# Second layer's gates activated in three sets (three, two and three) in place of four pairs

## The reference

```python
def odd_layer(x, norm_g, w_in, w_out, qn, kn, lq1, lk1, lq2, lk2, subln_g, cos, sin, lambda_init):
    h = rms_norm(x, norm_g)
    proj = h @ w_in
    q, k, v, gate = jnp.split(proj, [C_QK, 2 * C_QK, 2 * C_QK + C_W], axis=-1)   # 8 heads
    ...                                   # q and k: normalised, halves rotated; two scores a head
    o = differential_attention(q1, q2, k1, k2, v, lam)
    o = rms_norm(o, subln_g) * (1.0 - lambda_init)
    y = (o.reshape(b, s, C_W) * jax.nn.silu(gate)) @ w_out
    return x + y
```

## Time and profile before

| | |
|---|---|
| median of 3 runs | 1946.0 us (1945.42 to 1946.75) |
| the profiled execution's own time | 1947.44 us |
| its span in the trace | 1945.5 us |
| TensorE matmuls busy | 1916.6 us, 99% |
| VectorE busy | 1039.5 us, 53% |
| ScalarE busy | 999.3 us, 51% |
| GpSimd busy | 953.6 us, 49% |
| table loads on ScalarE | 37, of 1.283 us each |

### The profile page before, as it was taken

How to read it: one execution, slowest core, us unless ns; L and a number is a source line. 1 busy time by engine, 2 the same in 40 slices (tenths; PEclk the granted TensorE clock), 3 DMA queues, 4 the chain that set the end, 5 groups by cost and what they waited for, 6 DMA issues and landing times.

```text
span 1945.5 us, 27030 instructions
## 1 busy us (share of the span) xinstructions
PE 1916.6 (99%) x10082; PEld 1600.7 (82%) x10082; DVE 1039.5 (53%) x1882; ACT 999.3 (51%) x1767; POOL 953.6 (49%) x1238
## 2 busy tenths in 40 slices
PE   9999999999999999999999999999999999999998
PEld 7888787788788888888888888888878888888887
DVE  4376545756636766776565644312556574444214
ACT  5477546676725556665345444422656364444323
POOL 5642167555444444444555555555534355555553
PEclk9999999999999999999999999999999999999999
DMA  5321123322222222222222322333222122223332
GB/s 202 102 73 52 41 87 109 87 82 81 76 87 86 77 77 76 68 77 74 92 93 87 103 98 98 92 97 96 72 60 83 65 77 98 98 98 98 92 95 74
DMA packets 55380, 169.33 MB, mean 87 GB/s; under 512 B 7120, under 2 KB 14032, under 8 KB 55120
## 3 DMA queue, kind: packets, MB, share of 16 engines
q1 hardware_dynamic: 54960, 167.50, 27.5%
q10 hardware_dynamic: 288, 0.10, 0.0%
HBM read 158.66 MB, written 2.10 MB: 83 GB/s over the span
## 4 chain that ended last, share of the span: by engine, by line
PE 89%; DVE 6%; ACT 2%; POOL 1%; issue 1%; DMA 0%; SPq 0%; DVEq 0%; ACTq 0%
PE ps L2020 23%; PE ps L2023 22%; PE ps L2021 22%; PE ps L2076 3%; PE ps L2032 3%; PE ps L2033 2%; PE ps L2035 2%; PE ps L2091 2%; PE ps L2084 1%; PE ps L2060 1%; PE ps L2070 1%; PE ps L2174 1%; PE ps L2180 1%; PE ps L2150 1%; POOL wl L2768 1%
## 5 line engine op out<-in xcount | busy, mean ns | idle before, releaser
L2768 POOL TENSOR_TENSOR wl<-st,wh 128x256 fp32r<-128x256 f32 (+1 forms) x1164 | 871.7, 780 | 931.1 <-ACT wh L2198 930.6
L2020 PE MATMUL ps<-xh,wh 128*128 128x512 f32 x1416 | 577.1, 408 | 1.1 <-DVE tmp L2456 1.1
L2023 PE MATMUL ps<-xh,wl 128*128 128x512 f32 x1416 | 553.1, 391 | 0.0
L2021 PE MATMUL ps<-xl,wh 128*128 128x512 f32 x1416 | 552.4, 390 | 0.0
L2198 ACT ACTIVATE wh<-st 128x1024 fp32r<-128x1024 f32 (+3 forms) x307 | 309.6, 1010 | 457.8 <-PE ps L2023 410.0
L2020 PEld LDWEIGHTS ps<-xh,wh 128*128 128x128 f32 x1416 | 266.4, 188 | 57.5 <-issue 7.2
L2023 PEld LDWEIGHTS ps<-xh,wl 128*128 128x128 f32 x1416 | 265.8, 188 | 57.1
L2021 PEld LDWEIGHTS ps<-xl,wh 128*128 128x128 f32 x1416 | 266.6, 188 | 54.1 <-issue 5.5
L2727 DVE SCALAR_TENSOR_TENSOR tmp<-ps,vec,tmp 128x510 f32<-128x510 f32 (+1 forms) x176 | 131.1, 748 | 208.4 <-ACT tmp L2377 205.6
L2685 DVE SCALAR_TENSOR_TENSOR res<-res,ps 128x512 f32<-128x512 f32 (+1 forms) x37 | 22.7, 614 | 212.8 <-PE ps L2023 204.4
L2020 PE MATMUL ps<-fa_h,wh 128*128 128x512 f32 x308 | 119.9, 389 | 0.0
(11 more groups left out here) (326 smaller groups left out, 3431.4 us busy)
## 6 DMA issues: line engine op xcount, KB each, us to landing
st<-in_f_up SPq DMA_DIRECT2D x88, 512.0 KB, 3.2
st<-in_o_fm SPq DMA_DIRECT2D x32, 512.0 KB, 3.5
st<-in_s_xbc SPq DMA_DIRECT2D x32, 512.0 KB, 3.5
st<-in_f_dn SPq DMA_DIRECT2D x32, 512.0 KB, 3.5
st<-in_e_fm SPq DMA_DIRECT2D x21, 512.0 KB, 3.5
st<-in_s_z SPq DMA_DIRECT2D x16, 512.0 KB, 3.5
st<-in_s_out SPq DMA_DIRECT2D x16, 512.0 KB, 3.4
tmp<-tmp SPq DMA_DIRECT2D x100, 64.0 KB, 2.0
```

The costliest lines, as they stand in the source:

```text
L2020: e.matmul(u.bank.ap, hi, x.h[:, kk, :], start=first, stop=False)
L2021: e.matmul(u.bank.ap, hi, x.l[:, kk, :], start=False, stop=False)
L2023: e.matmul(u.bank.ap, lo, x.h[:, kk, :], start=False, stop=last).then_inc(S["mm"], 1)
L2768: e.tensor_tensor(P.mem["wl"][w.slot][:, part], P.mem["stage"][w.m % NSTAGE][:, part], P.mem["wh"][w.slot][:, part].bitcast(F32), ALU.subt ...
```

## The change

`Gates` gets a table `sets`: behind which gate's unit silus are done, and of which gates. The even layer's table says the same as the rule before it did, since only its gates 4 to 7 come through `bring`. In the odd layer the gates' units move to other heads, and their silus are done in three sets: gates 0, 1 and 2 behind gate 2's unit (head 1's units), gates 3 and 4 behind gate 4's (head 4's units), and gates 5, 6 and 7 behind gate 7's (head 7's units, the last ones of the stream).

```diff
@@ class Gates
         self.beside = {5: [4], 6: [5], 7: [6, 7]}
+        self.sets = {5: (4, 5), 7: (6, 7)}
 ...
     def bring(self, j, u):
         self.raw[j] = yield ("gate_in", self.sg[:, j, :], u, self.over)
         u.bank.release(self.raw[j])
-        if j % 2:
+        if j in self.sets:
             P = self.P
             P.put("table", "silu_and_others", [])
-            for i in (j - 1, j):
+            for i in self.sets[j]:
                 self.t[i] = P.put("gate_s", self.sg[:, i, :], self.raw[i])
             P.put("table", "natural_log_exp_and_others", [])
@@ odd_layer
     gates = Gates(P, mem["o_sg"], over)
-    gates.beside = {1: [0, 1], 3: [2, 3], 5: [4], 6: [5], 7: [6, 7]}
+    gates.beside = {1: [0, 1, 2], 4: [3, 4], 6: [5], 7: [6, 7]}
+    gates.sets = {2: (0, 1, 2), 4: (3, 4), 7: (5, 6, 7)}
```

## The result

The changed kernel takes **1955.2 us** (median of 5 runs, 1954.58 to 1955.80); the kernel before took 1946.75 us beside it (1945.42 to 1947.66). The ratio is 1.0044, 95% interval 1.0029 to 1.0059: slower, by 8.4 us. I had forecast 1952.4 us with a range up to 1954.8. The direction and the place were right; the time lies 0.4 us beyond the range.

The account below looks back on a forecast made before the run. TensorE, 99% busy, was taken as the bound, so only its waits, small extras and clock could move the time. -0.45 - 1.7 + 0.4 + 6.6 + 1.6 = +6.45 us gave 1952.4 us, range 1946.8 to 1954.8.

Parts of the forecast that it names:

- The end: +6.6: First output triple to block 7: 8.1 us of waits in place of 1.5; bounds +4.0 and +8.7.
- The wait for the bank, 0.4: Ahead of head 7's first scores: TensorE waits 0.4 us for an output bank freed by head 5's gating.
- one of the signs that I had named as showing me wrong: Layer's end: the forecast is wrong if head 7's scores start before gate 7's silu.
- Heads 1 to 6: -1.7 + 0.4 - 0.45 = -1.75: Old head 6 and 7 waits go, -1.7; heads 1 to 4 share fewer units, +0.4; fewer small-matmul groups, -0.45 us.
- the five groups: TensorE: five groups of small matmuls fewer have a triple behind them, 0.09 us each, -0.45 us.
- The wait for `kz` of head 7: TensorE's 0.8 us wait at head 7's first scores goes, part of the -1.7 us.
- The clock: +1.6: Layer's end: dense waits bring one fall of TensorE's clock, +1.6 us; bounds 0 and +3.2.
- My upper bound of 3.2: Clock term's upper bound: another fall behind the 2.5 us wait ahead of block 7, +3.2 us.
- Table loads: 0: ScalarE: two loads of 1.28 us go, hidden by TensorE's stream of triples, so nothing is counted.
- The base: Starting time: the profiled execution, 1947.44 us, taken as 1.4 above the median of the three runs.
- the signs that I named: Profile after: 35 loads, listed waits at the end, TensorE busy at most 15.5 of 20 us, low clock within 25 us.
- The rival at full clock, 1950.8 us: Layer's end: waits exposed but no fall of the clock, the sum without 1.6, 1950.8 us; chance 0.23.

Follow-up runs that it names:

- late_bank: Changed kernel, but the planner reserves a head's output bank only when two of its blocks' softmax are planned; 1951.1 us.
- old_units_567: Changed kernel with the gates' units where the kernel before had them, silu sets (0,1), (2,3), (4) and (5,6,7); 1954.2 us.
- filled_end: Changed kernel with only eight matmuls of zeros, ahead of block 7 of the output projection; 1952.9 us.
- before_both: Kernel before with the later output bank and eight matmuls meant for the last norm's wait, which landed at an unwaiting unit instead; 1952.4 us.
- more_loads: Kernel before, same order, with eight more table loads, two more in each of the odd layer's four pairs of silus; 1954.7 us.
- filled: Changed kernel with twenty matmuls of zeros in the waits of head 7 and ahead of block 7; 1951.5 us.
- sets_332: Changed kernel with three silu sets of 3, 3 and 2: gates 3, 4 and 5 behind head 4's units, 6 and 7 behind head 7's; 1952.1 us.
- five_alone: Changed kernel, but gate 5 gets its silu by itself behind its own unit; 1951.5 us.
- before_late_bank: Kernel before, but a head's output bank is taken only when two of its blocks' softmax are planned; 1950.8 us.
- late_bank_filled: Changed kernel with the later output bank and twenty matmuls of zeros in head 7 and ahead of block 7; 1952.7 us.
- after_bank: Changed kernel, but until head 7's last scores the output projection may use one of the two small-transpose banks; 1957.1 us.

## Why the prediction missed by a little

1. **The end: +6.6, measured about +7.0.** From the first output triple to block 7 I had 33.1 us; it took 33.55. The steps came at (forecast in brackets): scores of 128 keys 4.1 (4.5), of 384 keys 11.6 (11.8), of 512 keys 15.3 (15.1), third unit 19.7 (19.3), transpose 30.7 (30.3), block 7 33.6 (33.1). The wait for the bank, 0.4, did not come: the scores write other banks, and the head's output bank is only filled later. In its place are two waits of 0.47 and 0.58 us for a copy of the transposed probabilities, which I had only as part of a bound. That head 7 could not start before gate 7's silu was my condition; that it did was one of the signs that I had named as showing me wrong: head 7's scores start at 524.05, 0.1 us ahead of gate 7's silu. The rest of the chain came nearly where I had put it all the same, since the planner, not the chip, had placed it so late (`late_bank`).
2. **Heads 1 to 6: -1.7 + 0.4 - 0.45 = -1.75, measured about -2.5.** Block 7 starts 5.55 us later than before (553.52 against 547.97), of which 1.03 us were there from the program's start: this one execution had a fall of the clock at 12 us that the one before had not. That leaves 4.5; less 7.0 for the end it is -2.5. The waits account for 1.6 of it, the five groups for 0.45 by my estimate, and 0.4 I can't assign. The wait for `kz` of head 7 is gone, as forecast, and of head 2's, too.
3. **The clock: +1.6, measured 3.7 over the runs. This is the step that failed: the term was too small by more than half.** I took one fall. In the profile it is what the odd layer shows: the fall behind block 7, at 555.0, which cost 1.6 us. But the mean loss rose by 3.7 us (standard error 0.5), and filling the layer's waits brought back 3.7 us by the medians and 3.2 by the means. My upper bound of 3.2 was made of two falls at 1.6, where a fall can last 6.8 us, not 3.4. Where the rest of the 3.7 us lies stays open, since the changed kernel has one profile. There are two candidates. One is a second place inside head 7, where I had noted 4.7 us of waits in 7.5; there the clock falls in the profiles of old_units_567, filled_end and before_both. The other is outside the layer, where I had taken everything as unchanged: at 12 us (1.0 us later behind it, against the profile before) and near 1580 us (0.7 us later).
4. **Table loads: 0.** The two fewer show no gain that can be told apart. But my reason, that ScalarE idles half the time, was wrong: eight loads more cost 7.8 us. The first pair shows a load delaying what stands behind it on ScalarE, by 2.07 us, and with it a chain from exponentials to the next scores; the idle half did not help there. The page "ScalarE: Activation LUTs" of the Trainium skill (What ACT_TABLE_LOAD costs) puts load and drain at some 2.66 us. The traces disagree again: in more_loads three loads in a row start 1.29 us apart, and the silus 1.29 us behind the last.
5. **The base.** I counted from a median of 1946.0; the kernel before came to 1946.75 beside the changed one and to 1947.1 in more runs. That is 0.8 to 1.1 of the 2.8 us by which the forecast fell short. The clock's extra 2.1 less 0.6 for the waits makes 1.5; the 0.2 to 0.5 us left are within the error. Counted from 1946.75, the same sum gives 1953.2 with a range up to 1955.6, which holds the measured time: that it lies 0.4 us outside is owed to the base as much as to the clock.

Of the signs that I named, 35 loads, two waits of 1.23 us for the exponentials, 2.23 ahead of block 7, none for `kz` and 33 us and more were right. The output bank's wait was absent; TensorE was busy 15.9 of the first 20 us, where I had 15.5; and the shown stretch of low clock began 31 us behind head 7's first scores, not within 25. Head 7's scores did start ahead of gate 7's silu (item 1); the other two signs of being wrong, under 5 us of waits at the end and over 2 us won or lost in heads 1 to 4, did not come.

The rival at full clock, 1950.8 us, is what `filled` comes near to (1951.5): with the clock's part gone, the sum of the waits was good to a microsecond.

## What to carry to other kernels

Price a step by what stands right behind it on its engine and who waits for that, not by the engine's idle share: the same rearrangement that relieves ScalarE by two loads cost 4 us of waits because it put a head's softmax chain behind the stream's last unit. Where several waits of about a microsecond fall close together, or one of over 2 us, count what the clock may take as well, with a wide bound: against the kernel before, the loss grew by 0.4 times what the rest did in sets_332 and more_loads, by 0.9 times in the changed kernel and by 3.7 times in late_bank. One profile is not enough to say where it falls. An edit of a planner's resources has no sign of its own: the later output bank won 4.1 us on one kernel and lost 3.8 on its neighbour.

## What the runs showed of the hardware

- **The same wait did and did not bring a fall.** The 2.23 us ahead of block 7 were followed by a clock of 0.5 in the profiles of the changed kernel, old_units_567, five_alone and late_bank, and by none in those of sets_332, before_late_bank and before_both, at one profile each. The kernels before_late_bank and before_both have the same waits in head 7, 0.58 and 0.96 us, and only the second has a fall behind them. The wait of about 1.87 us ahead of the last norm's matmuls was followed by a fall in the profile of the kernel before (at 1569) and by none in that of late_bank_filled (at 1574). What decides it I could not say from the wait's length.
- **Here a fall lasted 3.4 us or twice that.** In the odd layer, over all profiles, seven were 3.4 us long and three 6.8 (in old_units_567, filled_end and after_bank).
- **The clock also falls where it costs nothing.** In every profile it is at 0.50 at the end of the span, behind TensorE's last matmul (in the changed kernel from 1947.7 us, the last matmul ending at 1944.2).
- **With matmuls of zeros in the waits, no fall came there.** In the one profile of `filled` its twenty, half of the array's rows and only zeros, went with a clock of 1.00 through the whole end, and they delayed nothing where they stood inside waits. Where they did not, in late_bank_filled, twelve of them cost 3.9 us.
